# Two-layer hybrid network on one core: the modulation vectors transposed on VectorE, and TensorE filled with matmuls on a constant before the first product

## The reference, cut to what matters

```
c_silu, cc_silu = silu(c), silu(c_ctx)                      # two vectors of 1024
shift_x, scale_x, gate_x = split(c_silu  @ ada_w + ada_b, 3)   # ada_w: 1024 x 3072 for each layer
shift_y, scale_y, gate_y = split(cc_silu @ ada_w + ada_b, 3)
hx = rms_norm(x, norm_w) * (1.0 + scale_x) + shift_x
hy = rms_norm(y, norm_w) * (1.0 + scale_y) + shift_y
... = split_cols(hx @ w_in), split_cols(hy @ w_in)             # the first products, then attention, retention, merge
x = x + gate_x * merge_branches(...)
```

## Time and profile before

| | |
|---|---|
| median of 3 runs (lowest to highest) | 2072.24 us (2070.7 to 2075.02) |
| profiled execution, its own time | 2075.69 us |
| its span, first to last instruction | 2074.0 us |
| mean granted TensorE clock | 0.982 |
| PE busy | 1985.5 us, 96% |
| PEld / DVE / ACT / POOL busy | 1777.9 / 1114.2 / 897.0 / 241.5 us |
| DMA | 289.23 MB, mean 139 GB/s |

### The profile page before, as it was taken

The page is one execution under the profiler, slowest core; times in us unless marked ns, Lnnn a source line. Parts: engine busy times, 40 slices in busy tenths (PEclk is TensorE's granted clock), DMA queues, the critical chain, the costliest instruction groups (busy, mean ns, idle before and its releaser), DMA issues.

```text
span 2074.0 us, 36747 instructions
## 1 busy us (share of the span) xinstructions
PE 1985.5 (96%) x14016; PEld 1777.9 (86%) x14016; DVE 1114.2 (54%) x1790; ACT 897.0 (43%) x1443; POOL 241.5 (12%) x268
## 2 busy tenths in 40 slices
PE   6999999999999899999998999989999999999998
PEld 4777777777787688888898999979999999999998
DVE  4554443345532654545655555775556555676554
ACT  4444232234332544434544444554444444554443
POOL 1000110101011100201121001220001000200000
PEclk9999999999999899999998999989999999999999
DMA  7221343411124332342354555335555555445553
GB/s 293 79 69 62 132 151 121 136 56 66 63 95 148 108 97 93 111 133 95 120 175 144 186 184 182 117 124 178 182 183 193 183 182 183 153 145 181 182 182 112
DMA packets 79429, 289.23 MB, mean 139 GB/s; under 512 B 8912, under 2 KB 9168, under 8 KB 79312
## 3 DMA queue, kind: packets, MB, share of 16 engines
q1 hardware_dynamic: 77616, 281.61, 40.9%
q0 software_dynamic: 1120, 4.72, 0.7%
q10 hardware_dynamic: 576, 1.24, 0.2%
HBM read 286.49 MB, written 1.05 MB: 139 GB/s over the span
## 4 chain that ended last, share of the span: by engine, by line
PE 56%; DVE 5%; ACT 3%; issue 2%; POOL 1%; POOLq 0%; DVEq 0%; ACTq 0%
PE bank L2243 18%; PE bank L2245 17%; PE bank L2244 17%; DVE w_lo L1752 1%; ACT w_hi L1475 1%; PE bank L2445 1%; PE bank L2428 1%; PE bank L2414 1%; PE bank L2386 0%; ACT h_hi L1491 0%; PE bank L2485 0%; PE bank L2368 0%; DVE r_conv L2176 0%; ACT m L1505 0%; DVE h_lo L1836 0%
## 5 line engine op out<-in xcount | busy, mean ns | idle before, releaser
L2243 PE MATMUL bank<-h_hi,w_hi 128*128 128x256 f32 (+1 forms) x2720 | 871.0, 320 | 21.8 <-DVE h_lo L1836 7.6
L2245 PE MATMUL bank<-h_hi,w_lo 128*128 128x256 f32 (+1 forms) x2720 | 847.6, 312 | 0.0
L2244 PE MATMUL bank<-h_lo,w_hi 128*128 128x256 f32 (+1 forms) x2720 | 846.5, 311 | 0.0
L1752 DVE TENSOR_TENSOR w_lo<-raw,w_hi 128x1024 fp32r<-128x1024 f32 x484 | 596.1, 1235 | 418.4 <-ACT w_hi L1475 417.9
L1475 ACT ACTIVATE w_hi<-raw 128x1024 fp32r<-128x1024 f32 x484 | 508.9, 1055 | 508.2 <-PE bank L2245 448.8
L2243 PEld LDWEIGHTS bank<-h_hi,w_hi 128*128 128x128 f32 x2720 | 519.5, 191 | 84.3 <-issue 45.7
L2245 PEld LDWEIGHTS bank<-h_hi,w_lo 128*128 128x128 f32 x2720 | 519.7, 191 | 28.8
L2244 PEld LDWEIGHTS bank<-h_lo,w_hi 128*128 128x128 f32 x2720 | 520.7, 191 | 22.9
L2243 PE MATMUL bank<-hid_hi,w_hi 128*128 128x256 f32 x704 | 198.1, 281 | 2.1 <-DVE hid_lo L2099 2.1
L2245 PE MATMUL bank<-hid_hi,w_lo 128*128 128x256 f32 x704 | 197.5, 281 | 0.0
L2244 PE MATMUL bank<-hid_lo,w_hi 128*128 128x256 f32 x704 | 197.2, 280 | 0.0
(11 more groups left out here) (235 smaller groups left out, 2141.9 us busy)
## 6 DMA issues: line engine op xcount, KB each, us to landing
raw<-in_weights SPq DMA_DIRECT2D x516, 512.0 KB, 3.3
early<-in_first SPq DMA_DIRECT2D x10, 512.0 KB, 13.1
bias<-in_rpb POOLq DMA_DIRECT2D x8, 384.0 KB, 3.4
early_o<-in_first SPq DMA_DIRECT2D x4, 512.0 KB, 15.7
x<-in_tokens SPq DMA_DIRECT2D x2, 512.0 KB, 6.1
x<-in_tokens ACTq DMA_DIRECT2D x2, 512.0 KB, 8.4
work<-in_first SPq DMA_DIRECT2D x2, 512.0 KB, 15.9
out<-cols_out SPq DMA_DIRECT2D x4, 256.0 KB, 2.5
```

What stands on the lines that cost most here:

```text
L1752: dve.tensor_tensor(w_lo[:, t % RAW, :], raw[:, t % RAW, :], w_hi[:, SPLIT_NO[t] % SPLIT, :].bitcast(F32), ALU.subtract).then_inc(lo_ready, 1)
L2243: nc.tensor.matmul(dst, w_hi[:, SPLIT_NO[t] % SPLIT, at], hi, start=start, stop=False, skip_group_check=shared)
L2244: nc.tensor.matmul(dst, w_hi[:, SPLIT_NO[t] % SPLIT, at], lo, start=False, stop=False, skip_group_check=shared)
L2245: return nc.tensor.matmul(dst, w_lo[:, t % RAW, at], hi, start=False, stop=stop, skip_group_check=shared)
```

## The change

Every array strip gets its own 32 columns of each 128 and sums over all 1024 rows, so nothing is left to add across strips. For a pair that is 4 matmuls of 64 moving columns (32 shift, 32 scale) for each of the 8 row blocks, 32 matmuls in place of 8; for a section tile 4 of 256 columns in place of 2 of 512. DVE then transposes 32x32 blocks of the bank straight from PSUM into SBUF (128x64 for a pair, 128x256 for a section) and adds the bias. ACT's copies, PE's `pair_turn` and `ada_turn` and the constant `parts` go.

A new step `busy` issues matmuls of 512 columns on a block of ones into bank `G[0]`, whose result nobody reads: 38 before pair 0, 7 before `norm_mean`, and 3 each after pairs 2, 3, 4 and 5. The ones lie in the fourth `w_hi` buffer, which POOL sets first of all. The hand-written order is changed so that `prescale` and `normed` of a chunk stand nearer to each other, and pair 7 comes after the first part of the first product together with `normed` of chunks 6 and 7.

```diff
-CONSTS = [("ident", P), ("ones", 1), ("heads", 2), ("parts", 2),
+CONSTS = [("ident", P), ("ones", 1), ("heads", 2),
           ("swap", P), ("cos", SEQ), ("sin", SEQ), ("dif", 3 * P), ("window", GRID_W)]
-EARLY = P + 5
+EARLY = P + 3
...
+    def keep_busy(self, n):
+        self.add("busy", part=n)
...
-        s.add("ada_rows", u=done)
-        def turn():
-            done.m = s.use("M")
-            s.add("ada_turn", u=done)
-        s.later(2, turn)
+        s.later(1, lambda: s.add("ada_turn", u=done))
...
-    pairs = {}
     def pair(k):
-        pairs[k] = s.add("ada_pair", k=k, t_use=s.use("T"))
-    def turn(k):
-        s.add("pair_turn", u=pairs[k], k=k, m=s.use("M"))
+        s.add("ada_pair", k=k, t_use=s.use("T"))
     def scale(*ks):
         for k in ks:
             prescale(s, norm, k)
+    s.keep_busy(38)
     pair(0)
+    s.keep_busy(7)
     norm_mean(s, norm)
     pair(1)
     s.add("split", t=SPLIT_TILES[0])
     norm_spread(s, norm)
-    turn(0)
+    scale(0, 1)
     pair(2)
-    turn(1)
-    scale(0, 1)
-    turn(2)
+    s.keep_busy(3)
+    normed(s, norm, 0)
     scale(2)
-    normed(s, norm, 0)
+    normed(s, norm, 1)
+    scale(3)
     pair(3)
-    turn(3)
-    scale(3, 4)
-    normed(s, norm, 1)
+    s.keep_busy(3)
     normed(s, norm, 2)
+    scale(4)
+    pair(4)
+    s.keep_busy(3)
+    normed(s, norm, 3)
     scale(5)
-    pair(4)
-    turn(4)
+    pair(5)
+    s.keep_busy(3)
+    normed(s, norm, 4)
     scale(6)
-    normed(s, norm, 3)
+    pair(6)
+    normed(s, norm, 5)
     scale(7)
-    pair(5)
-    turn(5)
-    normed(s, norm, 4)
-    pair(6)
-    turn(6)
-    normed(s, norm, 5)
     def last_pair():
+        normed(s, norm, 6)
         pair(7)
-        turn(7)
-        normed(s, norm, 6)
-    def last_chunk():
         normed(s, norm, 7)
         s.hold = False
         s.split_ahead(0)
-    s.background = [last_pair, last_chunk]
+    s.background = [last_pair]
...
-        pair_rows = merge_tanh[:, :, 0:SEQ]
-        ada_rows = [merge_tanh[:, 0, :], bias[:, :, :, :].rearrange("p a b c -> p (a b c)")[:, 0:BOTH]]
+        turned_m = merge_tanh[:, 0, 0:SEQ]
+        turned_b = bias[:, 0, 0, 0:SEQ]
...
+            pool.memset(w_hi[:, SPLIT - 1, 0:BOTH].bitcast(F32), 1.0).then_inc(set_up_busy, 1)
             pool.memset(c_silu[:, :, :], 0.0).then_inc(c_zero, 1)
...
-            def ada_pair_step(st):
...
-            def ada_rows_step(st):
...
-                    act.wait_ge(m_free, layer_1_turn[1].m + 1)
+                    act.wait_ge(ada_set, sections[1, 0])
...
-            def pair_turn_step(st):
+            def ada_pair_step(st):
                 k = st.k
-                dve.wait_ge(m_full, st.m + 1)
-                if k == 0:
+                dve.wait_ge(t_full, st.t_use + 1)
+                if k:
+                    dve.wait_ge(ada_set, k)
+                else:
                     dve.wait_ge(par_landed, 16)
+                dve.transpose(turned_m[:, 0:2 * 32], T[st.t_use % 2][:, 0:2 * 32]).then_inc(t_free[st.t_use % 2], 1)
+                dve.wait_ge(*t_out(st.t_use))
                 at, nw = PARAM_AT["ada_b"], PARAM_AT["norm_w"] + k
                 b = par[:, at:at + 2 * KC].rearrange("p (c k) -> p c k", c=2)[:, :, k].unsqueeze(2).to_broadcast([P, 2, 2])
                 dst = ada[:, 0, 0:2 * KC, :].rearrange("p (c k) j -> p c k j", c=2)[:, :, k, :]
-                dve.tensor_tensor(dst, M[:, 0:4].rearrange("p (c j) -> p c j", c=2), b, ALU.add).then_inc(m_free, 1)
-                dve.wait_ge(m_free, st.m + 1)
+                dve.tensor_tensor(dst, turned_m[:, 0:2 * 32].rearrange("p (c q) -> p c q", c=2)[:, :, 0:2], b, ALU.add)\
+                    .then_inc(ada_set, 1)
+                dve.wait_ge(ada_set, k + 1)
                 dve.scalar_tensor_tensor(out=ada_a[:, k, :], in0=ada[:, 0, KC + k, :], scalar=1.0,
                                          in1=par[:, nw:nw + 1].to_broadcast([P, 2]), op0=ALU.add, op1=ALU.mult)\
                     .then_inc(a_ready, 1)
...
-                dve.wait_ge(m_full, u.m + 1)
-                dve.wait_ge(par_landed, 16)
-                b = par[:, at:at + KC].rearrange("p (h c) -> p h c", h=2).unsqueeze(3).to_broadcast([P, 2, 4, 2])
-                dst = ada[:, u.layer, KC * u.c:KC * u.c + KC, :].rearrange("p (h c) j -> p h c j", h=2)
-                sums = M[:, :].rearrange("p (c q h z) -> p q h c z", c=4, q=2, h=2)
-                dve.tensor_tensor(dst, sums[:, 0, :, :, 0:2], b, ALU.add).then_inc(ada_part, 1)
-                dve.wait_ge(ada_part, u.n + 1)
-                dve.tensor_tensor(dst, sums[:, 1, :, :, 0:2], dst, ALU.add).then_inc(m_free, 1)
-                if u.c == 1:
-                    ada_m[u.layer] = u.m + 1
-            ada_m = [0, 0]
+                dve.wait_ge(tile_used, u.tile + 1)
+                dve.wait_ge(ada_set, KC + st.n)
+                turned = turned_m if (u.layer, u.c) == ADA_LAST else turned_b
+                dve.transpose(turned, T[u.t_use % 2][:, 0:SEQ]).then_inc(t_free[u.t_use % 2], 1)
+                dve.wait_ge(*t_out(u.t_use))
+                b = par[:, at:at + KC].unsqueeze(2).to_broadcast([P, KC, 2])
+                dve.tensor_tensor(ada[:, u.layer, KC * u.c:KC * u.c + KC, :],
+                                  turned.rearrange("p (k q) -> p k q", k=KC)[:, :, 0:2], b, ALU.add).then_inc(ada_set, 1)
...
+            def busy_step(st):
+                if st.n == 0:
+                    pe.wait_ge(set_up_busy, 1)
+                ones = w_hi[:, SPLIT - 1, 0:BOTH]
+                for _ in range(st.part):
+                    nc.tensor.matmul(G[0][:, :], ones[:, 0:P], ones, start=True, stop=True)
...
-                for j in range(2):
-                    strip = 32 * (2 * (k % 2) + j)
-                    ins = nc.tensor.matmul(T[u.t_use % 2][strip:strip + 32, :], c_silu[:, k, :],
-                                           raw[:, st.tile % RAW, 512 * j:512 * j + 512], start=(k < 2),
-                                           stop=(k >= KC - 2), skip_group_check=True)
-                    if j == 0 and k == KC - 1:
+                columns = raw[:, st.tile % RAW, :].rearrange("p (k g q) -> p g k q", k=KC, g=4)
+                for g in range(4):
+                    ins = nc.tensor.matmul(T[u.t_use % 2][32 * g:32 * g + 32, 0:SEQ], c_silu[:, k, :], columns[:, g, :, :],
+                                           start=(k == 0), stop=(k == KC - 1), skip_group_check=True)
+                    if g == 0 and k == KC - 1:
                         ins.then_inc(t_full, 1)
...
-                    strip = 32 * (i % 4)
                     rows = first_tiles[2 * k + i // 4][:, SEQ * (i % 4):SEQ * (i % 4) + SEQ]
-                    ins = nc.tensor.matmul(T[use % 2][strip:strip + 32, 0:SEQ], c_silu[:, i, :], rows, start=(i < 4),
-                                           stop=(i >= 4), skip_group_check=True)
+                    columns = rows.rearrange("p (c g q) -> p g c q", c=2, g=4)
+                    for g in range(4):
+                        ins = nc.tensor.matmul(T[use % 2][32 * g:32 * g + 32, 0:2 * 32], c_silu[:, i, :], columns[:, g, :, :],
+                                               start=(i == 0), stop=(i == KC - 1), skip_group_check=True)
                 ins.then_inc(t_full, 1)
-            def pair_turn_step(st):
...
-            def ada_turn_step(st):
```

More of the change, by code:

```diff
@@ L1098, in block_kernel @@
         c_zero = sem("c_zero")
-        ada_part = sem("ada_part")
+        ada_set = sem("ada_set")
+        set_up_busy = sem("set_up_busy")
         prescaled = sem("prescaled")
@@ L1236, in block_kernel @@
         v_jobs = [st.job for st in steps if st.kind == "sg_v"]
-        layer_1_turn = {st.u.layer: st.u for st in steps if st.kind == "ada_turn" and st.u.c == 0}
+        sections = {(st.u.layer, st.u.c): KC + st.n + 1 for st in steps if st.kind == "ada_turn"}
         block = ctx.enter_context(nc.Block())
@@ L1446, in split_step @@
                 split(st.t, None)
-            def ada_pair_step(st):
-                act.wait_ge(t_full, st.t_use + 1)
-                nc.scalar.activation(pair_rows[:, st.k % 2, :], T[st.t_use % 2][:, 0:SEQ], ACT.Copy)\
-                    .then_inc(t_free[st.t_use % 2], 1)
-            def ada_rows_step(st):
[L1456 to L1463, removed]
             def split(t, r):
@@ L1714, in sg_mix_step @@
                 mix_split(st.c, KC + st.n)
-            run = {"split": split_step, "ada_pair": ada_pair_step, "ada_rows": ada_rows_step, "square": square_step,
+            run = {"split": split_step, "square": square_step,
                    "normed": normed_step, "evacuate": evacuate_step, "value_rows": value_rows_step,
@@ L2221, in _ @@
             run = {"split": lambda st: split(st.t), "add_square": add_square_step, "prescale": prescale_step,
-                   "pair_turn": pair_turn_step, "ada_turn": ada_turn_step, "ada_scale": ada_scale_step, "norm_mean": norm_mean_step,
```

(27 more changed lines are left out.)

5 lines of the change are left out of this document (1 added, 4 removed).

## The result

The changed kernel takes 2060.60 us (median of 5 runs, 2058.06 to 2062.58), the one before 2072.24 (2070.70 to 2075.02). The medians differ by 11.6 us. The ratio taken over the single runs, which isn't the quotient of the medians, is 0.9938 with a 95% interval of 0.9924 to 0.9951, or 10.2 to 15.7 us less. The profiled execution took 2060.16 us, its span is 2058.4.

What follows compares the result with a forecast made beforehand. Bound taken: in the setup a serial PE-ACT-PE loop at the low clock, later PE. Setup 12.0 plus stream 1.1 is 13.1 us off the profiled 2075.69, 2062.6; the median lies 3.45 lower, 2059.1 us; range 2054 to 2069.

Steps and rivals of the forecast that it cites:

- The burst: 38 fill matmuls before pair 0: about 12 slow, 26 fast, ending at 12.7 us as pair 0's data lands; cost about 0.
- A pair on PE: Setup: 64 records in place of 16 for a pair, taken as 1.5 us, 2.2 at the low clock.
- rival C: Small matmuls cost by their number; at 0.112 us a record a pair takes 7.2 us, total 2106; chance 0.07.
- Mean and spread: Setup: the mean's records take 1.8 us, not 3.5, ending at 17.7; `rstd` at 21.8 in place of 24.41, 2.6 us.
- DVE's part of a pair: Setup: transpose 0.22 us, with two additions 0.55 us for a pair; 1.5 us of each round goes.
- DVE the bound behind `rstd`: Setup: DVE's queue of 17.8 us ends at 39.6, second product starts at 41.2 in place of 53.22, 12.0 us gained.
- PE keeps up if a pair costs under 2.0 us: Setup: with pairs at 1.5 us PE's side comes to 37.7 us, under DVE's 41.2, so PE does not bound.
- the forecast's sum for PE: Setup: 27.2 us plus seven pair times to the second product, with 4.0 us behind pair 7 for DVE, ACT, `h_lo` and split.
- The stream: Product stream after the setup: three section transposes of 0.36 us leave PE, 1.1 us gained.
- Section tiles: Product stream: 16 records in place of 8 for two tiles, same array time, 1.06 us; change taken as 0.
- rival E: The second product starts early, but the stream meets something unmoved, such as the bias tables; then 2071 us; chance 0.07.
- Rival B: The clock falls back and rounds run slow from pair 1; second product at 51.2, 2069 us, priced at 2066; chance 0.22.

Runs made afterwards that it cites:

- e1: The changed kernel with all six `keep_busy` calls, its 57 fill matmuls, taken out; 2065.18 us, ratio 0.9953 to the kernel before.
- e6: The changed kernel with only 8 of 16 `ada_w` tiles loaded, pairs 4 to 7 reusing them, and weight tiles 1 to 5 asked for after pair 6; 2057.74 us, one run.
- e4: The changed kernel with each of the four fills of 3 matmuls of 512 columns cut into 12 of 128 columns; 2061.42 us, ratio 0.9947.
- e5: The changed kernel with 4 fp32 fill matmuls before pair 0 in place of all 57, and the constant `parts` put back; 2059.72 us, ratio 0.9945.
- e7: The changed kernel with 34 fills plus 32 matmuls of a pair's shape in place of the 38 before pair 0; 2062.89 us, ratio 0.9946.
- e2: The kernel before with only the same 57 fill matmuls added, keeping its own order of pairs and turns; 2067.91 us, ratio 0.9964.
- e8: As e7, but without the four fills of 3 matmuls between the pairs; 2065.79 us, ratio 0.9954.

## Why the prediction was right, step by step

The forecast was 2059.1 us, measured are 2060.6; 13.1 us were predicted to go, 11.6 went. The mechanism is the forecast one, DVE as the bound behind an earlier `rstd`; that the number came so near is in part luck, as an `rstd` 1.3 us earlier than forecast and waits of 2.0 us that the forecast hadn't lie on opposite sides.

*The burst.* Predicted end 12.7; it ended at 12.50, with the rise some 5 us in. Right.

*A pair on PE.* Taken 1.5 us from bounds of 1.0 and 7.2; it takes 1.10 at the full clock and 1.93 in e1 at the low one, the same as 16 records with four times the columns. So 64 loads and 64 issues cost nothing: 17 ns a record, and rival C is out. The short window in the earlier trace rows was the right row, though misread: of its four records one is the mean's last (18.94 to 19.29), so three of the pair start within 0.02 us, not four within 0.04. By the Trainium skill ("TensorE: Matmul & The Clock Gate", the section on why the gap is 56 ns) it would have been about 62 ns a record, an estimated 4.0 us for a pair; that figure is for hardware decoding off, how it was set here no trace shows, and the measured 17 ns is far from it.

*Mean and spread.* `rstd` predicted at 21.8, there at 20.53: 3.9 us earlier in place of 2.6. The mean took the predicted 1.8 us, but started at 15.18, and its last records ended before 17.0 in place of 17.7; DVE's pair step and `w_lo` then stood in front of the copy as predicted.

*DVE's part of a pair.* 0.55 us predicted, with 0.22 for the transpose; the transpose takes 0.24 and the step 0.56 (26.27 to 26.82). Right.

*DVE the bound behind `rstd`.* This is the term that was mis-sized. The queue itself is 17.56 us (e1) and 17.54 (e6) against 17.8, but in the changed kernel 19.70 pass, as "PE keeps up if a pair costs under 2.0 us" didn't hold for each single pair: PE was far ahead on average, and stood still for 1.95 us in pair 6, which put 1.03 us on DVE, and 0.93 more in pair 7, which stands in order behind six product matmuls at 0.43 and runs at 1.42 itself, the clock having fallen in the stop (that last link is read from the rows, not tested by itself). `rstd` gave 1.3 more than forecast and these waits took 2.0: the last `h_lo` ended at 40.23, predicted 39.6. Behind it `w_lo` of tile 1 was ready 1.4 us later (predicted 1.6), and PE, which still had 18 product matmuls to do from 37.46, came to the second product at 42.04, 0.4 later than that. So the last step was PE's, not DVE's: the forecast's sum for PE had 4.0 us behind pair 7 for DVE and ACT, and not these 18 matmuls (4.6 us with a third stop of 0.17). 12.0 us were predicted there and 11.2 came. That an early stop is a matter of instructions and not of data is shown by e4, e5 and e7 (the stop moves with the count of instructions, 127 records apart) and by e6 (it goes with the load on the DMA).

*The stream.* Three turns at 0.36, 1.1 us. Compared with the kernel before at the same groups of PE, the lead grows by 0.45 us over the first section turn (9.05 at 256 us, 9.50 at 287), and between there and 402 us by 0.69 more than in e2, which keeps the turns: 1.14. Section tiles at 0, row of the kernel after below, against 1.06: right.

```profile
204.47 1.07 PE L2270 MATMUL bank<-raw,c_silu 128*32 128x256 f32 x16
...
112.00:114.00 2.00, 2.00 (x5) 1.56 (x6) 1.41 (x6) 1.04 (x5) 0.00 (x0) 0.50 0.03 8
```

*Given back (rival E), a little.* Two steps of 0.3 us are lost, between 77 and 86 us and between 112 and 121, in every kernel with the shorter table of constants, and in neither of the two that keep `parts` (e2: 6.68, 6.67; e5: 10.93, 10.93). That it goes with the table's layout is shown; by what mechanism is open. So 11.2 - 0.6 + 1.1 = 11.7, and the medians differ by 11.6; with an interval of 10.2 to 15.7 us on the measured gain an agreement to 0.1 is chance.

*What is no effect of the change.* The second row above is a fall of the clock in the middle of the stream, 1.5 us, at a place where no other kernel here has it; the kernel before has one of about 2 us near 380. They come and go between executions, which is why the profiled spans (15.6 us apart) are no measure of the change.

*The clock's share.* Rival B had the rounds slow, with their fills in them, and the second product at 51.2. No run is slow throughout with the fills in, so that price stays untested. In the changed kernel the clock did fall, but only behind the stop in pair 6, and it was up again by 38 us (0.23 from 37.80 to 38.03). In e1 there are no fills, most of the setup and pairs 5 and 6 are slow, and the second product starts at 42.33; by the estimate there, slow pairs alone would not hold DVE. The forecast named clock and transposes together and didn't split them; the runs do: at the second product the transposes and the new order are worth 10.9 us alone, the fills 0.3 on top of them (0.6 at 63 us). The medians alone don't settle it: the intervals of e1 and of the change overlap.

## What to carry to other kernels

Price the two halves of a change also one without the other: a clock that is raised is worth little where another engine is the bound, and the 38 + 7 + 12 matmuls on a constant brought 0.3 to 0.6 us here by the markers, which the times don't tell from nothing. Where a step is replaced by many small instructions, count them against the stretch of full DMA that they run in, and not only against the array: take the records between two stops that no semaphore ends. A bound by averages ("a pair under 2 us keeps up") needs the largest single stop added where the consumer has no work queued.

## What the runs showed of the hardware

- **PE's instructions come in blocks, and under a full DMA they come late.** In the rounds of pairs PE stopped 127 matmul records with their loads apart: for 0.76 and 1.95 us (after), 1.06 and 2.58 (e4), 1.43 and 2.28 (e5), up to 3.00 (e8), at some 400 GB/s; with 122 GB/s there was no stop inside a pair (e6). The page has 89 packets in the queue `q8 instruction`, against 85 for the kernel before; 521 more matmuls with their loads are 1042 instructions, 4.1 blocks of 254. The Trainium skill ("Runtime: NRT & Kernel Launch", the section on instruction fetch mechanics) has blocks of 256 instructions, which agrees with the 254 counted here to within two, and calls the crossing of one mostly hidden, which holds in e6 and not in the setup here.
- **A stopped PE can lose its clock as well**: 1.95 us without work, and the windows behind read 0.86, 0.50 and 0.79 (32 to 38 us); 512 columns took 0.43 us again. Behind the 2.42 us stop of e8 the clock stayed up for the next 100 records, so not each stop does it.
- **Four strips of 32 columns run as one**: 64 records of 64 columns in 1.10 us. With the whole array as weights and 128 columns it is otherwise: 12 matmuls took 1.56 us (e4), 0.125 us each (20.73 to the next pair's 22.23), where a quarter of the 0.23 us for 512 columns is 0.06.
- **VectorE transposes 128x64 fp32 out of PSUM in 0.24 us** (8 records, 0.241 to 0.250).
- **POOL's addition and DVE's `w_lo` nearly took turns**: while POOL added a bias (2.11 us from 41.27), the second `w_lo` took 2.89 us (from 41.57) where the first took 1.23. In e4 and e8 it was the first, with the second product waiting for it. In e6 a `w_lo` had started first, at 41.98: it took 1.22 us, and POOL's addition from 42.18 took 2.73, where it took 1.53 in the kernel before with no `w_lo` beside it. The one that started later paid.
